# Reordering a block-triangular solve: two pairs of groups a level and a half apart

## What is computed

```python
def step(state, inp):
    r_t, w_t, k_t, v_t, a_t, b_t = inp
    sa = jnp.einsum('bhij,bhj->bhi', state, a_t)
    state = (state * w_t[:, :, None, :] + sa[..., None] * b_t[:, :, None, :]
             + v_t[..., None] * k_t[:, :, None, :])
    y_t = jnp.einsum('bhij,bhj->bhi', state, r_t)
    return state, y_t
```

## Time and profile before

| | us |
|---|---|
| median of three runs | 1047.98 |
| lowest, highest | 1045.89, 1052.87 |
| the profiled execution | 1053.86 |
| its span, first to last instruction | 1052.0 |

### The profile page before, as it was taken

The page is one execution under the profiler, slowest core; times in us unless marked ns, Lnnn a source line. Parts: engine busy times, 40 slices in busy tenths (PEclk is TensorE's granted clock), DMA queues, the critical chain, the costliest instruction groups (busy, mean ns, idle before and its releaser), DMA issues.

```text
span 1052.0 us, 17877 instructions
## 1 busy us (share of the span) xinstructions
PE 1006.5 (96%) x7758; PEld 643.3 (61%) x7758; DVE 528.7 (50%) x807; ACT 319.2 (30%) x584; POOL 131.2 (12%) x152
## 2 busy tenths in 40 slices
PE   8999999988888999999999999999999999999998
PEld 7777899978785678778788443344444444444343
DVE  4568852245536876575665433344333333433354
ACT  5467742153526751331233121111111111111110
POOL 0000000378934500000000100000000000000000
PEclk9999999998979999999999999999999999999999
DMA  9632021000004057466588899999999999999994
GB/s 386 244 116 112 2 81 44 11 5 3 4 3 161 1 187 282 134 224 221 199 359 333 335 408 418 426 427 428 426 426 427 426 426 426 426 429 418 416 416 174
DMA packets 42975, 273.24 MB, mean 260 GB/s; under 512 B 8032, under 2 KB 8176, under 8 KB 28688
## 3 DMA queue, kind: packets, MB, share of 16 engines
q1 hardware_dynamic: 39488, 264.42, 62.2%
q0 software_dynamic: 2400, 4.28, 1.2%
q10 hardware_dynamic: 1008, 3.38, 0.8%
HBM read 272.06 MB, written 4.19 MB: 263 GB/s over the span
## 4 chain that ended last, share of the span: by engine, by line
PE 81%; DMA 8%; DVE 7%; ACT 3%; issue 1%; SPq 0%; DVEq 0%; POOLq 0%; ACTq 0%
PE banks L1742 29%; PE banks L2285 18%; PE banks L2299 9%; DMA w_tok<-in_w 4%; DMA w_qkv<-in_w 3%; PE banks L2323 2%; PE banks L2324 2%; PE banks L2291 2%; PE banks L2271 1%; ACT xT L951 1%; PE banks L1905 1%; PE banks L1922 1%; PE banks L1920 1%; DVE ring L1362 1%; PE banks L1880 1%
## 5 line engine op out<-in xcount | busy, mean ns | idle before, releaser
L1621 DVE TENSOR_TENSOR hid<-banks,silu_a 64x512 f32<-64x512 f32 x32 | 22.2, 693 | 196.5 <-ACT silu_a L956 196.5
L2299 PE MATMUL banks<-w_ring,hidT 128*64 128x512 f32 x512 | 116.8, 598 | 1.1 <-ACT hidT L960 1.1
L1608 DVE SCALAR_TENSOR_TENSOR mod<-banks,row_weight,mod 64x512 f32<-64x512 f32 x64 | 47.9, 748 | 70.3 <-PE banks L2299 69.3
L2285 PE MATMUL banks<-w_tok,xT 128*64 128x512 f32 x176 | 80.0, 606 | 2.1 <-DMA w_ring<-in_w 2.1
L956 ACT ACTIVATE silu_a<-banks 64x512 f32<-64x512 f32 x32 | 19.0, 592 | 205.2 <-PE banks L2286 205.2
L2286 PE MATMUL banks<-w_ring,xT 128*64 128x512 f32 x176 | 80.0, 606 | 0.0
L1615 DVE TENSOR_TENSOR x<-x,banks 128x1024 f32<-128x1024 f32 x60 | 71.8, 1220 | 12.6 <-PE banks L2324 12.2
L2286 PE MATMUL banks<-w_tok,xT 128*64 128x512 f32 x176 | 77.9, 595 | 0.0
L2299 PEld LDWEIGHTS banks<-w_ring,hidT 128*64 128x64 f32 x512 | 34.3, 136 | 67.2 <-issue 65.9
L1742 PE MATMUL banks<-x_r,ring_r 128*128 128x512 f32 x192 | 74.8, 390 | 0.0
L2285 PE MATMUL banks<-w_ring,xT 128*64 128x512 f32 x160 | 70.8, 595 | 1.7 <-DMA w_qkv<-in_w 1.7
(11 more groups left out here) (386 smaller groups left out, 2195.8 us busy)
## 6 DMA issues: line engine op xcount, KB each, us to landing
w_ring<-in_w SPq DMA_DIRECT2D x42, 2048.0 KB, 24.3
w_tok<-in_w SPq DMA_DIRECT2D x16, 2048.0 KB, 25.4
ada_buf<-in_w_ada SPq DMA_DIRECT2D x64, 256.0 KB, 3.5
w_ab<-in_w SPq DMA_DIRECT2D x8, 2048.0 KB, 25.5
w_qkv<-in_w SPq DMA_DIRECT2D x7, 2048.0 KB, 28.7
w_tok<-in_w SPq DMA_DIRECT2D x24, 512.0 KB, 17.1
w_ring<-in_w SPq DMA_DIRECT2D x24, 512.0 KB, 17.7
w_ring<-in_w SPq DMA_DIRECT2D x10, 1024.0 KB, 15.2
```

The source lines that it names most:

```text
L1608: dve.scalar_tensor_tensor(dst[:, 512 * n:512 * n + 512], bank[5][SLOTS * n:SLOTS * n + SLOTS, :], weight_of(e), gate2[:, n, :], ALU.mult, ...
L1621: dve.tensor_tensor(hid[:, :], bank[3][SLOTS:P, :], silu_a[:, :], ALU.mult).then_inc(hid_v, 1)
L2285: pe.matmul(bank[2][0:SLOTS, :], rows, w1_of(k), start=(k == 0), stop=(k == KT - 1))
L2299: mm = pe.matmul(bank[5][SLOTS * n:SLOTS * n + SLOTS, :], hidT[:, k, :], w2[:, k, 512 * n:512 * n + 512], start=(k == 0), stop=(k == 3))
```

## The change

Pair a is groups 0 and 1, pair b groups 2 and 3. All the products stay. What moves:

- Pair b starts behind pair a's `r1`: it runs a level and a half behind pair a, where it was half a level behind. Only the forms of pair a are masked at the start of a half; those of pair b are masked between pair a's masks of levels 1 and 2. The six unread matmuls ahead of group 2's `t0` go.
- Pair a's outputs, and in the first half the forms of the second half for groups 0 and 1, stand among pair b's last steps (`m5`, `wu`, `gh`). Pair b's chain and outputs of the first half stand among pair a's first steps of the second half (`t0`, `x`, `r0`, `p1`).
- The four small decay copies stand ahead of the solve. The decay table is made in four pieces of one quarter each, two in each half, between masks of the levels. The state factors wait for their own piece.
- The first state is written by ScalarE straight from PSUM, two copies of 64x256, in place of VectorE's copy from the ring; `outputs(0, 0)` now waits for it.
- ScalarE takes a square root of a constant behind the first `end_keys`; the square root that GpSimd waits for stands behind pair a's `h`, and VectorE's reciprocal behind `queries_added(0, 0)`.

The names `first_inverse`, `level_masked` and `state_factors` hold the operations of L1308, L1310 and L1314, one group at a time. `out_copy` holds L795 to L797.

ScalarE's stream:

```diff
+def state_start():
+    for k in pair_a:
+        ins = act.activation(STATE[HD:P, 4 * k:4 * k + 4, :].rearrange("p h n -> p (h n)"), bank[2 * k + 1][HD:P, 0:256], ACT.Copy)
+    ins.then_inc(chain_v, 1)
+
+def out_copy(half, n):
+    at = 4 * half + n
+    act.wait_ge(out_y, at + 1)
...
+for k in range(NG):
+    end_keys(0, k)
+act.activation(small[:, 57:58], one, ACT.Sqrt)
 for half in range(2):
-    for k in range(NG):
-        end_keys(half, k)
-    solve_copy(half, "x", 0, 1)
...
+    solve_copy(half, "x", *pair_a)
+    if half:
+        out_copy(0, 2)
+    solve_copy(half, "r0", *pair_a)
+    if half:
+        out_copy(0, 3)
+        for k in pair_b:
+            end_keys(1, k)
+    solve_copy(half, "n1", *pair_a)
+    solve_copy(half, "r1", *pair_a)
+    solve_copy(half, "x", *pair_b)
+    solve_copy(half, "r0", *pair_b)
+    for n in range(2, 5):
+        solve_copy(half, f"n{n}", *pair_a)
+        solve_copy(half, f"r{n}", *pair_a)
+        solve_copy(half, f"n{n - 1}", *pair_b)
+        solve_copy(half, f"r{n - 1}", *pair_b)
+    solve_copy(half, "m5", *pair_a)
+    solve_copy(half, "wu", *pair_a)
+    solve_copy(half, "n4", *pair_b)
+    solve_copy(half, "r4", *pair_b)
+    solve_copy(half, "h", *pair_a)
     if half == 0:
+        state_start()
         act.wait_ge(ssq_qk, 1)
         act.activation(rms_qk, ssq, ACT.Sqrt).then_inc(sqrt_qk, 1)
+    out_copy(half, 0)
+    solve_copy(half, "m5", *pair_b)
+    out_copy(half, 1)
+    solve_copy(half, "wu", *pair_b)
+    solve_copy(half, "h", *pair_b)
     if half == 0:
+        for k in pair_a:
+            end_keys(1, k)
         act.activation(ident_bf, ident, ACT.Copy)
         act.activation(mask_bf, const("diag_mask"), ACT.Copy)
+out_copy(1, 2)
+out_copy(1, 3)
```

VectorE's stream:

```diff
+for half in range(2):
...
-    dve.tensor_tensor(DECAYS.rearrange("p s h n -> p (s h) n"), const("eye2").unsqueeze(1).to_broadcast([P, TT * HEADS, CH]),
...
+def chunk_decays(sc):
+    dve.tensor_tensor(DECAYS[:, sc], const("eye2").unsqueeze(1).to_broadcast([P, HEADS, CH]),
+                      decay_end2[:, sc, :].unsqueeze(2).to_broadcast([P, HEADS, CH]), ALU.mult).then_inc(s_de2, 1)
 def next_state(half, n):
...
-    if at == 0:
-        dve.tensor_copy(new, HH_OF[n // 2][to]).then_inc(chain_v, 1)
...
+masked_forms(0, 0)
+masked_forms(0, 1)
 for half in range(2):
+    first_inverse(half, *pair_a)
+    if half:
+        queries_added(0, 3)
+        next_state(0, 2)
+        next_state(0, 3)
+    level_masked(half, 1, *pair_a)
+    for k in pair_b:
+        masked_forms(half, k)
+    level_masked(half, 2, *pair_a)
+    first_inverse(half, *pair_b)
+    for n in range(1, 4):
+        level_masked(half, n, *pair_b)
+        level_masked(half, n + 2, *pair_a)
+        if n < 3:
+            chunk_decays(2 * half + n - 1)
+    level_masked(half, 4, *pair_b)
+    state_factors(half, *pair_a)
+    queries_added(half, 1 - half)
+    level_masked(half, 5, *pair_b)
+    queries_added(half, half)
+    if half == 0:
+        dve.wait_ge(sqrt_qk, 1)
+        dve.reciprocal(ssq, rms_qk).then_inc(rstd_qk, 1)
+        next_state(0, 1)
+        masked_forms(1, 0)
+        masked_forms(1, 1)
+    else:
+        next_state(1, 0)
+        next_state(1, 1)
+    state_factors(half, *pair_b)
+    queries_added(half, 2)
+next_state(1, 2)
+queries_added(1, 3)
```

TensorE's stream, behind the four `forms(0, k)`, which stay:

```diff
 for half in range(2):
-    for k in range(NG):
-        if half == 0 and k < NG - 1:
+    for k in pair_a:
+        if half == 0:
             pe.wait_ge(solve_v[k], v_at(0, "tt"))
             between(bank[2 * k][:, 256:256 + P], 6)
         solve_step(half, "t0", k)
-    solve_step(half, "x", *first_pair)
...
+    if half:
+        chain(0, 2)
+    solve_step(half, "x", *pair_a)
+    if half:
+        outputs(0, 2)
+    solve_step(half, "r0", *pair_a)
+    if half:
+        chain(0, 3)
+    solve_step(half, "p1", *pair_a)
+    if half:
+        outputs(0, 3)
+        forms(1, 2)
+        forms(1, 3)
+    solve_step(half, "n1", *pair_a)
+    solve_step(half, "r1", *pair_a)
+    solve_step(half, "t0", *pair_b)
+    solve_step(half, "p2", *pair_a)
+    solve_step(half, "x", *pair_b)
+    solve_step(half, "r0", *pair_b)
+    for n in range(2, 5):
+        solve_step(half, f"n{n}", *pair_a)
+        solve_step(half, f"p{n - 1}", *pair_b)
+        solve_step(half, f"r{n}", *pair_a)
+        solve_step(half, f"n{n - 1}", *pair_b)
+        solve_step(half, f"p{n + 1}", *pair_a)
+        solve_step(half, f"r{n - 1}", *pair_b)
+    solve_step(half, "m5", *pair_a)
+    solve_step(half, "p4", *pair_b)
+    solve_step(half, "wu", *pair_a)
+    solve_step(half, "n4", *pair_b)
+    solve_step(half, "gh", *pair_a)
+    solve_step(half, "r4", *pair_b)
+    solve_step(half, "p5", *pair_b)
+    if half == 0:
+        outputs(0, 0)
+        solve_step(0, "m5", *pair_b)
+        chain(0, 1)
+        outputs(0, 1)
+        forms(1, 0)
+        solve_step(0, "wu", *pair_b)
+        forms(1, 1)
+        solve_step(0, "gh", *pair_b)
+    else:
+        chain(1, 0)
+        outputs(1, 0)
+        solve_step(1, "m5", *pair_b)
+        chain(1, 1)
+        outputs(1, 1)
+        solve_step(1, "wu", *pair_b)
+        solve_step(1, "gh", *pair_b)
+chain(1, 2)
+outputs(1, 2)
+outputs(1, 3)
```

More of the change, by code:

```diff
@@ L1247, in _ @@
                 cut_first("att", n, 1)
+            for half in range(2):
+                for c in range(2):
+                    ins = dve.tensor_copy(decay_end2[HD * c:HD * c + HD, :, half::2],
+                                          decay_end[HD * half:HD * half + HD, :, c::2].rearrange("p t s -> p s t"))
+            ins.then_inc(s_de2, 1)
+            dve.wait_ge(s_de2, 1)
             dve.wait_ge(att_mm, 12)
@@ new lines, in first_inverse, with level_masked @@
+            def first_inverse(half, *groups):
+                for k in groups:
+                    dve.wait_ge(solve_mm[k], mm_at(half, "t0"))
+                    dve.tensor_tensor(INV[k], f4(bank[2 * k][:, 0:256]), bc4("level0"), ALU.mult).then_inc(solve_v[k], 1)
+            def level_masked(half, n, *groups):
+                for k in groups:
+                    dve.wait_ge(solve_mm[k], mm_at(half, f"p{n}"))
+                    dve.tensor_tensor(PP[k].rearrange("p (a c) n -> p a c n", c=2), banks[k][:, :, 0:128].rearrange("p c (a n) -> p a c n", a=2),
+                                      const(f"level{n}").unsqueeze(1).unsqueeze(1).to_broadcast([P, 2, 2, CH]), ALU.mult).then_inc(solve_v[k], 1)
@@ new lines, in state_factors @@
+            def state_factors(half, *groups):
+                for k in groups:
+                    sc, g = 2 * half + k // 2, k % 2
+                    dve.wait_ge(solve_mm[k], mm_at(half, "gh"))
+                    dve.wait_ge(s_de2, 2 + sc)
+                    dve.tensor_tensor(GG[k], f4(bank[2 * k][:, 256:512]), DECAYS[:, sc, 4 * g:4 * g + 4, :], ALU.add).then_inc(solve_v[k], 1)
+            masked_forms(0, 0)
+            masked_forms(0, 1)
+            for half in range(2):
+                first_inverse(half, *pair_a)
+                if half:
@@ L1329, in _ @@
+                level_masked(half, 4, *pair_b)
[7 more added lines that the diff above has]
+                    next_state(0, 1)
                     masked_forms(1, 0)
-                    next_state(0, 3)
-                    for k in range(1, NG):
-                        masked_forms(1, k)
-                else:
-                    queries_added(1, 0)
-                    queries_added(1, 1)
+                    masked_forms(1, 1)
+                else:
@@ L1956, in outputs @@
                 pe.wait_ge(solve_a[n], a_at(half, "h"))
-                pe.wait_ge(chain_v, at)
+                pe.wait_ge(chain_v, max(at, 1))
                 for k in (2 * (n // 2), 2 * (n // 2) + 1):
@@ L2021, in _ @@
                     forms(1, 3)
-                else:
-                    for n in range(4):
-                        if n < 3:
-                            chain(1, n)
-                        outputs(1, n)
+                solve_step(half, "n1", *pair_a)
[27 more added lines that the diff above has]
+                    solve_step(0, "gh", *pair_b)
+                else:
+                    chain(1, 0)
[8 more added lines that the diff above has]
+            outputs(1, 3)
             def turn_qk(i):
```

89 lines of the change are left out of this document (5 added, 84 removed).

## The result

| | median us | runs | ratio to before, 95% |
|---|---|---|---|
| before | 1051.26 | 20 (1045.89 to 1057.42) | |
| after | 1044.80 | 20 (1042.84 to 1049.39) | 0.9941 [0.9924, 0.9958] |

The change makes the kernel 0.6% faster, about 6 us. The profiled execution of after took 1044.92 (span 1043.0); 1044.5 had been forecast for it. So by the two profiles the sum came out, and by the timed runs it did not. Of all the executions in this document one was slow, the profiled one of old_order_no_unread; it is not counted in that kernel's figures.

What follows compares the result with a forecast made beforehand. TensorE bounds the kernel; only the solve shortens, passed on in full. Idle -4.0, fill -1.5, table pieces and waits +1.5, clock -5.4: -9.4, 1044.5 us profiled, 1038.6 median; own range 1035 to 1042, with A and B 1031 to 1047.

Steps and rivals of the forecast that it cites:

- 10.1 for 14.1: -4.0: Whole solve: TensorE's idle time would fall from 14.1 to 10.1 us, a gain of 4.0.
- +1.5 of table pieces and unplaced waits: Solve: allowance of 1.5 us lost, 0.7 of it for decay table pieces slowed beside GpSimd's rotation.
- I take 12 cold us for 25.6: Solve: time at 1.2 GHz would fall from 25.6 to 12 us, at 0.39 lost each: -5.4.
- The fill of -1.5: Start of a half: dropping the third batch of six unread matmuls would save 1.5 us.
- 1.29 + 0.53 + 0.05 = 1.87 us for each of pair b's two masked forms: Starts of both halves: VectorE's time per masked form, for which TensorE's `t0` of groups 2 and 3 must wait.
- 0.7 us of idle for the second half's end: Second loop to pair b's last `gh`: TensorE would idle only 0.7 us on the way.
- The middle is denser: Middle of the solve: denser work, given as one reason for only 12 us at 1.2 GHz.
- The stretch at 224.5 goes with its cause: First half: the cold stretch (PEclk 0.76) behind TensorE's 2.7 us idle at 224.5 would vanish with that idle.
- (A): Rival, middle and tail: cold stretches stay, the clock gives nothing; -4.0, 1044.0 us; chance 0.20.
- (B): Rival: clock holds until the tail, some 3 cold us, no unplaced waits; -13.7, 1034.3 us; chance 0.17.
- (C): Rival, both loops: clock falls at pair b's `t0` in both halves; slower, +5.1, 1053.1 us; chance 0.04.
- (D): Rival: GpSimd's rotation becomes the bound, needing 12 us more delay; a delay of 15 makes -6, 1042; chance 0.02.

Runs made afterwards that it cites:

- old_order_no_unread: The kernel before without any of the unread matmuls in its solve; median 1048.11 us, ratio 0.9937 to before.
- no_rotation: The kernel after with GpSimd's rotation of queries and keys left out; one execution of 1042.66 us.
- old_tail_fill_alone: The kernel before with six unread matmuls added behind the last `gh`, nothing else; median 1046.11 us, ratio 0.9944 to before.
- old_order_no_stalls: The kernel before, pair order kept, with early decay copies, decay table in four pieces and early square root; median 1050.07 us, ratio 0.9968.
- after_again: The kernel after run again with no edit; median 1045.65 us, ratio 0.9951 to before.

## Why the prediction was right and wrong

**The size was right in the profile, the terms were not.** Idle time: "10.1 for 14.1: -4.0", with the +1.5 of table pieces and unplaced waits -2.5 net. Measured: -0.4. Clock: "I take 12 cold us for 25.6", -5.4. Measured: 8.6 cold us, -6.6 at 0.39. The fill of -1.5 went as said. These make 8.5 of the 9.3; the rest is within the rounding of PEclk. The two errors of opposite sign make a total that fits; that is luck, and no merit of the sum. The time forecast, 1038.6, failed by a further step, the one from the profile to the median (below).

**The step that failed: the durations of the walk between the loops.** The prediction wrote "1.29 + 0.53 + 0.05 = 1.87 us for each of pair b's two masked forms" and used it in both halves, though the same group of rows showed the addition at 1.20 beside the rotation, and the rotation runs through the whole second half. Contention between the two engines was then priced for the table's pieces alone (0.7), which cost 0.6 and 0.1: 1.26 and 0.79 against 0.68. no_rotation shows what was missed, 2.5 us. The ends above say how the stretching works here: an addition that meets a GpSimd operation already begun ends 0.28 to 0.29 behind it. That is the rule of the Trainium skill (SBUF — State Buffer, "Who interferes with whom"), whichever starts first holds the ports for its whole length; the traces agree in all eight additions of the second halves of before and after, in each of which GpSimd had begun first; no case here shows the other order. The prediction wrote that no row settled "whether by whole operations"; the trace of before did, in the rows shown above. The two additions of after were 0.98 and 0.86 us longer than alone, more than the 0.67 that it priced and less than its worst case of 1.27.

**A second step that failed: 0.7 us of idle for the second half's end.** It was 2.69, of which 1.46 is one "issue" gap. What makes these gaps is open; no run here tried it.

**The clock.** The solve came to 0.96 for "near 0.94", and the tail to 8.58, short but not "under 8". "The middle is denser" is not borne out by idle time, though its clock rose (0.91 from 250 to 268.81; before had 0.79 from 250 to 270). "The stretch at 224.5 goes with its cause" named a cause that the runs do not bear out. old_tail_fill_alone has the same table of 2.29 and the same wait there, and the stretch ran at 1.00, where before had 0.76. The wait can be followed by a fall and need not be. What comes back in the traces of the old order without the fill is the cold tail: 0.58 in before, 0.56 in old_order_no_stalls.

**The step that put the time wrong: from the profile to the median.** The forecast subtracted a profiled difference from the median of three runs. That median lay 3.3 below the median of twenty, which is half of the miss of 6.2; the other 2.9 are forecast gain that the timed runs do not show. The cold term of a single execution of before was 37.9 us where the mean of 29 is 32.4; after's was 16.7 against a mean of 18.9 to 21.0. That is 5.5 + 2.2 to 4.3 cold us, 3.2 to 4.1 us at 0.42, in the gain of 9.4 that other executions don't have. This covers what the timed gain falls short (6.5 for 9.4). The mean of before differs by group, 30.5 to 36.5 cold us, so the account is good to some 2 us only. The prediction had said that the profiled execution lay 5.9 above the median and did not ask what made it so.

**What the order gave.** Not fewer waits. At equal clock, after is about 1 us ahead of before (0.2 to 1.6); most of the rest of its 6 us is that its tail is short enough to lose less to the 1.2 GHz level: 0.73 of 8.58 is 4.6 cold us, 0.58 of 15.3 is 12.9, 3.5 us at 0.42. The old order's tail is 5.7 us longer cold than warm, and six matmuls get them back: behind a warm tail of 9.67, the new tail of 8.58 is worth 1.1. Ahead of the last `gh` both take 98.5 us (199.3 to 297.80; 199.5 to 298.07 with the stalls and the extra fill still in). These are single executions, but the pair of kernels with the six in the tail says the same: no gain by the order alone is shown.

**The rivals.** (A), cold stretches stay, and (B), the clock holds until the tail: neither; the cold us fell by two thirds, to 8.6 where (B) had 3, and some 4 of these lay ahead of the tail. (C), a fall at pair b's `t0` that lasts through the loops: no, both loops of after ran at 1.00, but a short fall did come there, 0.80 from 262 to 265.7 and 0.68 from there to the second loop; in after_again it came in the first half instead, 0.59 from 217.6 to 221.8. (D), the rotation as the bound: no by its end, 296.15 against 306.38 (it began at 241.96, forecast 240.1); it costs through VectorE's additions, a way that was no rival. The loops (220.65 to 230.89 for 220.2 to 230.3; 3.41 us a level for 3.36), the wait of `outputs(0, 0)`, the early table load and the free decay copies came as said.

## What to carry to other kernels

Take an operation's duration from where it will stand and from what runs beside it, not from the cleaner row. Before a tail of small serial products is reordered, look at the clock granted to it: a handful of unread matmuls in the wait ahead of it tests how much is clock. And ask of a profiled execution whether its clock is the usual one before its difference is taken from a median.

## What was not expected of the hardware

- The same kernel, undisturbed, gave times 12 us apart, and they follow the mean granted clock down to about 1.2 us (the scatter about the line of 29).
- An idle time of 2.7 us was followed by a granted clock of 0.76 in one execution and of 1.00 in another; unread matmuls raised the clock where they filled the wait ahead of a run of small products, and in the old order held it at the start of the solve too (1.00 for 0.76), where they cost more than that gave.
- GpSimd holds VectorE's two-input additions up to the end of its own operation: 0.43 us alone, 0.71 to 1.41 beside it, and always an end 0.28 to 0.29 behind the GpSimd operation.
